# Top scores of an indexer: float32 products against float32r products of high and low parts

## What is computed

```python
p = rmsnorm(x, g) @ w_in                     # and split by columns: ..., iq, ik, iw
rel = relu(einsum('bqhd,bsd->bqhs', iq, ik)) # 4 heads of 64 features, 1024 keys
score = einsum('bqh,bqhs->bqs', iw, rel) * idx_scale
score = where(admissible, score, -inf)       # keys of later chunks of 64 are out
top_val, top_idx = top_k(score, 256)
# attention runs over the chosen keys; next to it stand an mLSTM and a gated linear
# recurrence over other columns of p; all are joined and go through w_out
```

## Time and profile before

| | us |
|---|---|
| median of 3 runs | 3203.73 |
| the runs | 3203.73, 3208.0, 3203.65 |
| the profiled execution | 3206.39 |
| its span | 3204.8 |
| PE busy (share of the span) | 3004.5 (94%) |
| DVE busy | 1595.0 (50%) |
| ACT busy | 1195.6 (37%) |
| POOL busy | 1042.7 (33%) |
| TensorE's mean granted clock, as a share of full speed | 0.976 |

### The profile page before, as it was taken

How to read it: one execution, slowest core, us unless ns; L and a number is a source line. 1 busy time by engine, 2 the same in 40 slices (tenths; PEclk the granted TensorE clock), 3 DMA queues, 4 the chain that set the end, 5 groups by cost and what they waited for, 6 DMA issues and landing times.

```text
span 3204.8 us, 49910 instructions
## 1 busy us (share of the span) xinstructions
PE 3004.5 (94%) x18148; PEld 2586.9 (81%) x18148; DVE 1595.0 (50%) x3075; ACT 1195.6 (37%) x2173; POOL 1042.7 (33%) x686
## 2 busy tenths in 40 slices
PE   5999895999999999998999999999998999999999
PEld 5688863777888888787999877997896989988877
DVE  2699935623222322223019377981213828878861
ACT  3311146424222211223124356771322637666750
POOL 2123111252322325553226103434231543432325
PEclk9999997999999999999999999999999999999999
DMA  2223222331111112351287434314335861231223
GB/s 101 79 95 135 75 73 49 103 112 66 46 52 46 46 52 91 112 177 73 95 191 218 129 104 96 95 41 130 130 122 185 221 171 53 85 86 40 62 102 126
DMA packets 224151, 325.68 MB, mean 102 GB/s; under 512 B 81319, under 2 KB 167207, under 8 KB 221815
## 3 DMA queue, kind: packets, MB, share of 16 engines
q1 hardware_dynamic: 188838, 277.29, 28.7%
q10 hardware_dynamic: 33360, 39.98, 3.6%
q0 software_dynamic: 1792, 6.29, 0.7%
HBM read 229.95 MB, written 93.57 MB: 101 GB/s over the span
## 4 chain that ended last, share of the span: by engine, by line
PE 72%; DVE 6%; ACT 3%; issue 2%; POOL 2%; POOLq 0%; DMA 0%; DVEq 0%; ACTq 0%
PE psum L485 15%; PE psum L2209 15%; PE psum L2412 7%; PE psum L1998 7%; PE psum L1067 6%; PE psum L1036 6%; PE psum L1047 5%; PE psum L750 2%; PE psum L727 2%; DVE arena L2810 1%; PE psum L739 1%; PE psum L1082 1%; POOL out_ring L1988 1%; PE psum L3148 1%; PE psum L2849 1%
## 5 line engine op out<-in xcount | busy, mean ns | idle before, releaser
L2209 PE MATMUL psum<-parts_ffn 128*128 128x512 f32 x2112 | 482.8, 391 | 3.6 <-DVE parts_ffn L2166 3.6
L2209 PEld LDWEIGHTS psum<-parts_ffn 128*128 128x128 f32 x2112 | 398.7, 189 | 87.4 <-issue 2.2
L485 PE MATMUL psum<-parts_even,parts_ffn 128*128 128x256 f32 x2496 | 306.1, 285 | 5.2 <-DVE parts_ffn L2546 4.0
L485 PEld LDWEIGHTS psum<-parts_even,parts_ffn 128*128 128x128 f32 x2496 | 303.8, 194 | 5.9 <-DVE parts_ffn L2546 4.5
L485 PE MATMUL psum<-parts_odd 128*128 128x248 f32 x2304 | 277.3, 283 | 18.8 <-ACT arena L525 16.3
L485 PEld LDWEIGHTS psum<-parts_odd 128*128 128x128 f32 x2304 | 273.9, 193 | 21.4 <-ACT arena L525 15.3
L2279 DVE SCALAR_TENSOR_TENSOR arena<-psum,arena 128x1023 f32<-128x1023 f32 x88 | 112.9, 1283 | 329.9 <-ACT arena L2263 323.6
L525 ACT ACTIVATE arena<-psum 128x256 f32<-128x256 f32 (+2 forms) x240 | 87.4, 376 | 442.7 <-PE psum L485 438.2
L412 PE MATMUL psum<-parts_mixer 128*128 128x512 f32 x912 | 210.2, 393 | 3.9 <-DVE parts_mixer L271 3.9
L412 PEld LDWEIGHTS psum<-parts_mixer 128*128 128x128 f32 x912 | 173.0, 190 | 40.7 <-issue 4.6
L1109 ACT ACTIVATE both<-psum 128x512 fp32r<-128x512 f32 x256 | 140.1, 596 | 107.6 <-PE psum L1047 107.0
(11 more groups left out here) (339 smaller groups left out, 5805.1 us busy)
## 6 DMA issues: line engine op xcount, KB each, us to landing
arena<-ffn_up_b SPq DMA_DIRECT2D x44, 512.0 KB, 3.2
arena<-ffn_down_k SPq DMA_DIRECT2D x44, 512.0 KB, 3.5
arena<-x SPq DMA_DIRECT2D x10, 2048.0 KB, 8.6
arena<-w_in_e SPq DMA_DIRECT2D x13, 1024.0 KB, 6.6
e_tokens<-arena ACTq DMA_DIRECT2D x26, 512.0 KB, 3.1
x<-arena SPq DMA_DIRECT2D x24, 512.0 KB, 4.8
arena<-w_in_o SPq DMA_DIRECT2D x12, 992.0 KB, 6.2
o_tokens<-arena ACTq DMA_DIRECT2D x24, 496.0 KB, 3.0
```

Of the source, the lines that this page charges most:

```text
L485: last = pe.matmul(self.bank(t), self.hT[:, a, k, t * P:(t + 1) * P], self.weights.parts[:, self.weights.slot(s), b, k, :], start=(k, a, b ...
L2209: last = pe.matmul(self.core.psum[:, 4 * u + 2 * s + h, :], parts[:, s, a, k, :], self.hT[:, b, k, h * HALF:(h + 1) * HALF], start=(k, a, ...
```

## The change

TopScores multiplies in float32r. Keys and queries are loaded twice, into the lower and the upper 64 partitions. ACT copies the keys to float32r (`k_high`, 128 partitions), and the queries too, in two halves of 512 tokens (`q_parts`). DVE subtracts: `k_low` is the keys less `k_high` on all partitions, and the upper 64 partitions of `q_parts` become the queries less their high part. So one contraction over 128 rows sums high and low parts of the queries, and each piece takes two matmuls, with `k_high` and with `k_low`, into the same bank. A piece is at least 256 columns wide. POOL's two memsets of the buffers go. PE waits for the low parts of the keys and of the queries' first half before tile 0 and for the second half before tile 4. The new buffers lie where feat0's raw weights were (`k_high`, `k_low`) and in four free rows above (`q_parts`); the mLSTM's first two gate rows change places with others, since they are loaded during the scores.

```diff
-        self.rows = [core.take(S)[0:H] for n in range(8)]
+        spots = [core.take(S)[0:H] for n in range(8)]
+        self.rows = [spots[n] for n in (2, 3, 0, 1, 4, 5, 6, 7)]
...
+        self.k_high, self.k_low = (core.placed(f"{name}_{n}", parts_at + S * j, S, F32R) for j, n in enumerate(("k_high", "k_low")))
+        self.q_parts = shaped(core.placed(f"{name}_q_parts", parts_at + 4 * S, H * S, F32R), (H, S))
...
     def gpsimd(self, pool):
         hold(pool, self.after + self.splits_done)
-        pool.memset(self.qs[self.DH:P].rearrange("p a b -> p (a b)"), 0.0).then_inc(self.zeroed, 1)
-        pool.memset(self.ks[self.DH:P], 0.0).then_inc(self.zeroed, 1)
-        pool.wait_ge(self.zeroed, 2)
-
         pool.memset(self.scores[0][:, P:2 * P], OUT_OF_REACH).then_inc(self.padded, 1)

     def sync(self, sp):
         hold(sp, self.loads_after)
-        sp.dma_start(self.ks[0:self.DH], self.ik).then_inc(self.loaded, 16)
-        sp.dma_start(self.qs[0:self.DH], self.iq.rearrange("(h d) t -> d h t", d=self.DH)).then_inc(self.loaded, 16)
+        for at in (0, self.DH):
+            sp.dma_start(self.ks[at:at + self.DH], self.ik).then_inc(self.loaded, 16)
+        for at in (0, self.DH):
+            sp.dma_start(self.qs[at:at + self.DH], self.iq.rearrange("(h d) t -> d h t", d=self.DH)).then_inc(self.loaded, 16)
         sp.dma_start(self.wrow, self.iw).then_inc(self.loaded, 16)

     def tensor(self, pe):
         hold(pe, self.banks_after)
-        pe.wait_ge(self.zeroed, 2)
-        pe.wait_ge(self.loaded, 48)
+        pe.wait_ge(self.loaded, 80)
...
         for t in range(TT):
             keys = (t + 1) * P
+            if t % 4 == 0:
+                pe.wait_ge(self.low_out, 2 + t // 4)
...
                 for b in range(0, keys, HALF):
-                    w = min(HALF, keys - b)
-                    last = pe.matmul(self.core.psum[:, 2 * (n % 2) + b // HALF, 0:w], self.qs[:, h, t * P:(t + 1) * P],
-                                     self.ks[:, b:b + w], start=True, stop=True)
+                    w = max(min(HALF, keys - b), 2 * P)
+                    for part in (self.k_high, self.k_low):
+                        last = pe.matmul(self.core.psum[:, 2 * (n % 2) + b // HALF, 0:w], self.q_parts[:, h, t * P:(t + 1) * P],
+                                         part[:, b:b + w], start=part is self.k_high, stop=part is self.k_low)
                 last.then_inc(self.scored, 1)

+    def halves(self):
+        for g in range(2):
+            here = slice(g * HALF, (g + 1) * HALF)
+            yield g, self.qs[:, :, here], self.q_parts[:, :, here]
+
     def scalar(self, act):
-        hold(act, self.after)
+        hold(act, self.after + self.splits_done)
+        act.wait_ge(self.loaded, 80)
+        act.activation(self.k_high, self.ks, ACT.Copy).then_inc(self.high_out, 1)
+        for g, whole, parts in self.halves():
+            act.activation(parts, whole, ACT.Copy).then_inc(self.high_out, 1)
...
     def vector(self, dve):
         hold(dve, self.after)
+        dve.wait_ge(self.high_out, 1)
+        dve.tensor_tensor(self.k_low, self.ks, self.k_high.bitcast(F32), ALU.subtract).then_inc(self.low_out, 1)
+        lower = slice(self.DH, P)
+        for g, whole, parts in self.halves():
+            dve.wait_ge(self.high_out, g + 2)
+            dve.tensor_tensor(parts[lower], whole[lower], parts[lower].bitcast(F32), ALU.subtract).then_inc(self.low_out, 1)
         dve.wait_ge(self.turned, 1)
```

More of the change, by code:

```diff
@@ L1626, with __init__ @@
     H, DH, CHUNK = 4, 64, 64
-    def __init__(self, core, name, iq, ik, iw, scores, after, loads_after, banks_after, splits_done):
+    def __init__(self, core, name, iq, ik, iw, scores, after, loads_after, banks_after, splits_done, parts_at):
         H = self.H
@@ L1638, in __init__ @@
         s = core.sem
-        self.zeroed, self.loaded = s(f"{name}_zeroed"), s(f"{name}_loaded")
+        self.loaded, self.high_out, self.low_out = s(f"{name}_loaded"), s(f"{name}_high_out"), s(f"{name}_low_out")
         self.turned, self.weights_ready = s(f"{name}_turned"), s(f"{name}_weights_ready")
@@ L3288, in build @@
         masks = [core.take(max(t + 1, 2) * P) for t in range(TT)]
-        base = core.top
+        core.top = base = (core.top + 7) // 8 * 8
         hT = core.take_parts(2, KT, S)
@@ L3300, in build @@
         scores = TopScores(core, "scores", feat[IQ:IQ + 256], feat[IK:IK + 64], feat[IW:IW + 4], masks, norm1.done,
-                           norm1.done + feat0.stored_blocks(3), feat0.taken_out, feat0.weights.raw_free())
+                           norm1.done + feat0.stored_blocks(3), feat0.taken_out, feat0.weights.raw_free(), base)
         feat1_place = core.top
```

## The result

The changed kernel takes 3217.03 us (median of 12 runs, 3211.43 to 3223.21), the kernel before in the same session 3207.61 (12 runs). The ratio is 1.0029, 95% interval 1.0020 to 1.0038: slower by 9.4 us (6.4 to 12.2). The forecast was +6.0 on 3203.73, and "within 0.2%" had nearly the chance of "slower". "After" is the changed kernel, "before" the one it was made from. The profiled execution of after takes 3215.05 us, its span 3213.4, where before had 3206.39 and 3204.8.

The account below looks back on a forecast made before the run. DVE's path to the mLSTM head loads was taken as the bound, on a schedule set by PE's start of feat1. That start's +5.7 and 0.3 for half clock gave +6.0 on 3203.73: 3209.7 us, range 3203.5 to 3216.

Parts of the forecast that it names:

- Cleared rows: POOL's two memsets of the buffers, run under feat0's matmuls: taking them away is worth nothing.
- Loads: Second load of k and q 6.4 us, feat0's store among them 1.3: last landing from 90.77 to 98.4.
- Splitting: ACT's copies and DVE's subtracts after the landing: DVE's first score goes from 92.31 to 106.0.
- Products: Scores in float32r: DVE sets the pace and takes 27.0 us, where it took 39.5 before.
- POOL against DVE: Two splits of POOL meet DVE's subtracts and scores and cost DVE 5.0 us, bounds 0 and 6.1.
- DVE's end 138.0: DVE's end of the scores: 106.0 + 27.0 + 5.0 = 138.0, against 131.81, +6.2.
- PE's slack of 5.3 us: At the mLSTM head loads PE's path is ready 5.3 us before DVE's, and this stays.
- the whole path behind moves with PE: +5.7: From feat1 on, DVE stays on POOL's schedule, which follows PE, so all later work shifts by +5.7 us.
- rival B: Selection's phase against POOL's casts turns for the worse, changed kernel always on the long side: +11 us, chance 0.19.
- C: Rival: selection's phase turns for the better, DVE at least 0.5 us earlier against PE: +0.7 us, chance 0.13.
- D: Rival: the halves load together, or POOL misses DVE in the scores: about -0.4 us, chance 0.10.
- E: Rival: PE's clock stays or falls to 1.2 GHz in the scores: +9 us, chance 0.14.

Follow-up runs that it names:

- e3: Changed kernel with keys and queries loaded only into the lower 64 partitions, the upper cleared by POOL, queries' low part left out: 3212.79 us, ratio 1.0012 to before.
- e4: Changed kernel with feat1's first two weight loads issued ahead of the scores' loads: 3216.21 us, ratio 1.0022 to before.
- e10: Kernel before with only the start of the raw weights rounded up to a multiple of eight words: 3213.66 us, ratio 1.0020 to before.
- e11: Changed kernel with the raw weights kept on their old alignment, the parts alone rounded up: 3215.98 us, ratio 1.0028 to before.
- e13: Changed kernel, raw weights on old alignment, feat1's first weight loads ahead of scores, scan's memset in softplus wait, lru gate load behind head loads: 3208.98 us, ratio 1.0005.
- e9: Kernel before with feat1's first weight loads ahead of scores, scan's memset in softplus wait, lru gate load behind head loads: 3202.61 us, ratio 0.9979.

## Why the prediction was wrong

Step by step:

- *Bound by DVE, PE's busy share misleading.* Right. A kernel with 5.7 us less PE work is slower.
- *Cleared rows, 0.* Right within the scatter: e3 clears them again, and its transposes start no later than in the kernels with one load.
- *Loads, the landing at 98.4.* Too late by 2.8: it was 95.62. I had charged 6.4 for the second halves and 1.3 for the store in their midst; measured are 6.0 for both over 16 profiles, 5.4 by e3 against after. The rate was nearly right (212 GB/s for the 205 I took; 1.31 MB at 212 are 6.2), so the store's 1.3 didn't come on top. The Trainium skill, page "SBUF — State Buffer", section "Can I just issue two DMAs to hit both halves?": by its "+6%" my estimate was 5.7 and the store. The trace agrees that the two halves don't load side by side (212 GB/s with both in the queue, 209 with one).
- *Splitting.* The subtracts are right (1.226 and 2.29 forecast, 1.23 and, by the group, 2.288 measured), ACT's copies too (1.9 forecast, 1.85 measured). The first score came 7.6 us behind the landing, as forecast, at 103.24.
- *Products, 27.0 us without POOL.* Too short by 2.0: e4 shows 29.0. The widths' own durations are right (0.353 to 1.287) and DVE's busy time is 24.0, where I had 24.8. What I missed is the idle time: 5.0 us in the stage, some 0.6 a tile, where my gaps and late ReLUs make 2.2.
- *POOL against DVE, 5.0.* 4.94 by e4.
- *DVE's end 138.0, feat1 134.8, loads 401.4.* Measured 137.22, 134.02, 401.56. The errors of the loads (-2.8) and of the products (+2.0) cancel in DVE's end: the number came out by luck. "Where it was 2.7" was a misreading: it took the weights' row at 129.08 for the first matmul, which is at 128.67 and 3.1 before DVE's end, as in after (3.2). "PE's slack of 5.3 us stays what it was" failed by 1.2: in the table's last column it is 6.62 for 5.46. This hid the 0.8 by which feat1 came early.

What failed stands in the last lines of the sum, in two steps.

First, the base: "I add the difference found to the median", 3203.73 of three runs. The kernel before has a median of 3207.13 to 3209.5 in the later sessions, 3207.61 beside after, with single runs from 3200.65 to 3216.66. The forecast's 3209.7 misses by 7.3 us, and 3.9 of these are the base.

Second, "the whole path behind moves with PE: +5.7", with a slack that stays. It misses 3.4 us (9.4 less 6.0). The profiles show where: the means of before and after differ by 6.5 us at feat1 and by 9.6 where PE starts the mLSTM. So 3.1 us arise between, at the head loads. The sum took before's profile, with its loads on DVE's side, for the kernel. Its two other profiles are on PE's side, and both of after's are on DVE's. The side is worth 3.5 us at the mLSTM and the slow subtract 1.1 more. This is rival B's step, which I had priced at 5.3 and given 0.19.

What puts after always on DVE's side is, as far as 18 profiles show, a term that the sum didn't have: the rounding of `base`. I had read that line of the diff as bookkeeping, worth nothing, and didn't even list it. It makes 19 subtracts longer by 0.38 us and four of 2048 columns by 0.81; all nine profiles with it are on DVE's side, and four of the nine without. e10 prices it at 6.4 us (3.5 to 9.3) on the kernel before. Set each ratio times 3208 against the shift at feat1: in the seven timed kernels with the rounded address the time grew by 2.8 to 6.5 us more than feat1 moved, 4.6 on the mean; in the six others by -1.8 to 4.5, mean 1.0. The difference is 3.6, good to about 2 (my estimate from these 13).

That the rounding makes the missing 3.4 is likely, not shown. The direct test, e11, speaks against it: its profile does give the 3 us back (273.7 us from feat1 to the mLSTM, PE's side), but its median gives back 0.3. And e13, unrounded too, is 8.4 us slower than e9, with feat1 5.9 later. Either the new scores cost 8 to 9 us by themselves, or e11's eight runs fell badly; the intervals allow both. More profiles of e11 would tell, and none were taken.

The other rivals: B's number (+11) came near the result, and its statement "always on the long side" is true of the changed kernel in both its profiles. Its reason, half a us of phase, isn't borne out: e11, with feat1 at +6.21, is on PE's side. C and D are out. Of E the clock part is true and the price isn't: PE ran at half the clock until 114 us, where the tiles are narrow, and had the full clock for the wide ones.

## What to carry to other kernels

A line of a diff that only moves buffers is an edit like any other: look up which instructions read what it moves, and whether their durations in the trace change with the address. Engines that lock each other out make a small instruction follow the other engine's schedule, so work added or saved ahead of it can vanish; find who sets the schedule before summing. A margin of 0.01 us in one profile is a coin on its edge: the same kernel fell on either side in three profiles, and the sides differ by 3.5 us on the mean. And where three runs are shown as the time before, a forecast of a few us stands on their draw as much as on the sum: take the difference for the statement, and widen for the base.

## What the runs showed of the hardware

- A subtract of POOL, 128x1024, f32 and fp32r read, fp32r written: 1999 to 2015 ns with the f32 operand two words past a multiple of eight (5482 or 5490 of the arena for feat0), 2393 to 2414 with it on one (5488) or four past it (5484), where no subtract meets DVE's scan; 128x2048: 3810 to 3821 against 4622 to 4628. The output's place was the same.
- Beside POOL's cast and subtract, a three-operand instruction of DVE, 0.353 us alone, took 1.88 on the mean of three, and POOL's cast, 1.04 to 1.10 in other places, took 2.13 beside DVE's subtract of two SBUF operands.
- In after's 7.49 us of idle PE's granted clock went from 1.00 (89 to 90 us) to 0.50 (from 91 us). It stayed there to 114 us, with PE busy 2.4 of 6 us and at the end 3.55 of 4, and was 1.00 from 117 us on, with PE busy 7.6 of 8 us.
- A small tensor_scalar of 128x6, 0.17 us alone, came to 0.36 to 0.62 on the mean of 31, by how POOL's split fell against it.
